# One-hot products divided over the two steps of a quad, and down products ahead of the next gates in every second step

## The reference, cut to what matters

```python
def expert_block(args):
    xb, e = args
    hid = jax.nn.silu(xb @ w_g[e]) * (xb @ w_u[e])
    return hid @ w_d[e]
```

## Time and profile before

| | us |
|---|---|
| median of 3 runs | 1539.75 (1538.67 to 1543.53) |
| the profiled execution, its own time | 1538.04 |
| its span, first to last instruction | 1536.0 |
| PE busy | 1249.5 (81%) |
| DVE busy | 654.8 (43%) |
| ACT busy | 457.5 (30%) |

### The profile page before, as it was taken

How to read it: one execution, slowest core, us unless ns; L and a number is a source line. 1 busy time by engine, 2 the same in 40 slices (tenths; PEclk the granted TensorE clock), 3 DMA queues, 4 the chain that set the end, 5 groups by cost and what they waited for, 6 DMA issues and landing times. The chain is left out here.

```text
span 1536.0 us, 21387 instructions
## 1 busy us (share of the span) xinstructions
PE 1249.5 (81%) x8548; PEld 947.1 (62%) x8548; DVE 654.8 (43%) x1369; ACT 457.5 (30%) x999; POOL 147.8 (10%) x117
## 2 busy tenths in 40 slices
PE   3799899899999739899987429978999668888871
PEld 1589655688888727665665229945899655554540
DVE  0534586364435663221210085476667652211112
ACT  1233266543342421100100145335665410100002
POOL 1301000011102320000000140000001200000002
PEclk9999989999999869999999759989999879999996
DMA  9942258732322105999999905338554229999994
GB/s 319 301 117 84 81 194 284 211 107 86 107 94 74 66 1 197 392 414 413 418 420 384 353 14 140 110 137 278 183 173 162 97 90 421 422 423 423 421 422 154
DMA packets 140762, 352.75 MB, mean 230 GB/s; under 512 B 34144, under 2 KB 95584, under 8 KB 115968
## 3 DMA queue, kind: packets, MB, share of 16 engines
q1 hardware_dynamic: 123424, 315.95, 55.7%
q10 hardware_dynamic: 14176, 24.96, 4.5%
q0 software_dynamic: 3072, 10.59, 1.8%
HBM read 329.44 MB, written 22.02 MB: 229 GB/s over the span
## 5 line engine op out<-in xcount | busy, mean ns | idle before, releaser
L1595 DVE TENSOR_TENSOR w_lo<-ring,w_hi 128x256 fp32r<-128x256 f32 x480 | 223.4, 478 | 267.0 <-ACT w_hi L1308 266.6
L1308 ACT ACTIVATE w_hi<-ring 128x256 fp32r<-128x256 f32 x480 | 197.1, 417 | 290.6 <-PE banks L852 260.2
L1073 PE MATMUL banks<-ring,arena 128*64 128x256 f32 x2048 | 233.8, 383 | 39.7 <-issue 21.7
L852 PE MATMUL banks<-h_hi,w_hi 128*128 128x512 f32 (+1 forms) x640 | 222.0, 347 | 13.8 <-DVE w_lo L1595 11.0
L1073 PEld LDWEIGHTS banks<-ring,arena 128*64 128x64 f32 x2048 | 156.5, 137 | 107.9 <-issue 35.9
L852 PE MATMUL banks<-h_lo,w_hi 128*128 128x512 f32 (+1 forms) x640 | 220.3, 344 | 0.0
L852 PE MATMUL banks<-h_hi,w_lo 128*128 128x512 f32 (+1 forms) x640 | 219.9, 344 | 0.0
L1087 PE MATMUL banks<-ring,att 128*64 128x512 f32 x512 | 118.6, 605 | 29.8 <-issue 19.8
L852 PEld LDWEIGHTS banks<-h_hi,w_hi 128*128 128x128 f32 x640 | 122.8, 192 | 30.3 <-DVE h_lo L1587 8.4
L852 PEld LDWEIGHTS banks<-h_hi,w_lo 128*128 128x128 f32 x640 | 122.8, 192 | 14.1
L852 PEld LDWEIGHTS banks<-h_lo,w_hi 128*128 128x128 f32 x640 | 122.9, 192 | 13.7
(11 more groups left out here) (186 smaller groups left out, 1648.5 us busy)
## 6 DMA issues: line engine op xcount, KB each, us to landing
ring<-in_w_e_gate SPq DMA_DIRECT2D x64, 1024.0 KB, 9.1
ring<-in_w_e_up SPq DMA_DIRECT2D x64, 1024.0 KB, 9.6
ring<-in_w_e_down SPq DMA_DIRECT2D x64, 1024.0 KB, 10.0
ring<-in_w_mod SPq DMA_DIRECT2D x48, 1024.0 KB, 5.6
ring<-in_w_in SPq DMA_DIRECT2D x38, 1024.0 KB, 8.4
expert_rows<-arena ACTq DMA_DIRECT2D x32, 512.0 KB, 8.1
ring<-in_w_o SPq DMA_DIRECT2D x8, 1024.0 KB, 5.0
ring<-in_w_branch SPq DMA_DIRECT2D x8, 640.0 KB, 4.7
```

Source lines behind the costliest of these rows:

```text
L852: ins = mm(out_ap, a, b, start=k == 0 and p_ == 0, stop=k == KD - 1 and p_ == 2)
L1073: ins = mm(banks[e * CAP:(e + 1) * CAP, bank, 0:DE], x[:, k, e * CAP:(e + 1) * CAP], w[:, k * DE:(k + 1) * DE], start=k == 0, stop=k == KD ...
L1308: fn(w_hi[:, u % AHEAD, :, :], chunk(key)[:, q * KU:(q + 1) * KU, :], ACT.Copy).then_inc(w_hi_ready, 1)
L1595: v.tensor_tensor(w_lo[:, u % AHEAD, :, :], chunk(key)[:, q * KU:(q + 1) * KU, :], w_hi[:, u % AHEAD, :, :].bitcast(F32), ALU.subtract).th ...
```

## The change

It touches `pair_step` on PE and on DVE and nothing else. The one-hot products of the next quad stood all in the even step of a quad (one ahead of the gates, two between them and the down products, one behind). Now two pieces stand in the even step and two in the odd one, both directly behind the transposes. In odd steps the down products of pair p now stand ahead of the gate and up products of pair p + 1; in even steps they stay behind them. On DVE the copies follow, and `select` for the quad after the next moves from the end of the even step to the end of the odd one. SP's and ACT's instructions keep their order.

```diff
             def pair_step(l, p, i=None):
                 d = p // 2 + 1
-                ahead = p % 2 == 0 and d < NQUAD
                 step_h(l, p, i)
-                if ahead:
-                    step_x(l, d, 0, i)
+                if d < NQUAD:
+                    step_x(l, d, 2 * (p % 2), i)
+                    step_x(l, d, 2 * (p % 2) + 1, i)
+                if p % 2:
+                    step_d(l, p, i)
                 if p + 1 < NPAIR:
                     step_gu(l, p + 1, i)
-                if ahead:
-                    step_x(l, d, 1, i)
-                    step_x(l, d, 2, i)
-                step_d(l, p, i)
-                if ahead:
-                    step_x(l, d, 3, i)
+                if p % 2 == 0:
+                    step_d(l, p, i)
...
             def pair_step(l, p, i=None):
                 d = p // 2 + 1
-                ahead = p % 2 == 0 and d < NQUAD
                 take_hidT(l, p, i)
-                if ahead:
-                    take_xT(l, d, 0, i)
+                if d < NQUAD:
+                    take_xT(l, d, 2 * (p % 2), i)
+                    take_xT(l, d, 2 * (p % 2) + 1, i)
                 if p + 1 < NPAIR:
                     take_hid(l, p + 1, i)
-                if ahead:
-                    for q in (1, 2, 3):
-                        take_xT(l, d, q, i)
-                    if d + 1 < NQUAD:
-                        select(l, d + 1, i)
+                if p % 2 and d + 1 < NQUAD:
+                    select(l, d + 1, i)
```

## The result

The changed kernel takes **1718.6 us** (median of 4 runs, 1716.1 to 1720.2), the kernel before 1541.6 us (median of 4 runs). The ratio is 1.114 (95% interval 1.110 to 1.118): slower by 177 us. Predicted were 1718 us. The profiled execution has a span of 1714.1 us, 178.1 more than before.

What follows compares the result with a forecast made beforehand. The prediction took DMA transfers to bound the expert stages. The profiled 1538.0 us plus 14 stalls of 12.76 us (178.6) gave 1716.7, and the median 1.7 above it 1718 us; own range 1700 to 1740, overall 1670 to 1760.

Steps and rivals of the forecast that it cites:

- What bounds the stage: Expert stages run at the pace of the transfers, 13.63 MB a quad at 416 to 423 GB/s.
- The drain in odd steps: DMA engines stand still from the last byte of downs(p) until gates(p+2): 12.76 us, 14 times, 178.6 us.
- the ends: At the start of the stage, new gates one piece of 2 us later; taken as 0, between -3 and +3.
- The terms of one stall: Last byte to down products 1.63, down products 3.59, gate products 3.86, issue to full rate 1.63; together 10.71 us.
- The clock: Odd steps' down products start at half speed after some 8 or 10 us idle: 2.05 us more per stall.
- Start and completion of a transfer: In each stall, 1.63 + 1.63 us by the rows; the skill page's 2.0 together would give 18 us less.
- Select hidden by the transfers: Even step: wait for select, about 2.5 us, covered by transfers; 0.9 us spare in layer 0, some 4 in layer 1.
- the drain with the clock up: Rival: odd-step stalls without cold starts, 14 x 10.71 = 150 us, total 1690 us; chance 0.17.
- The longer one: Rival: 4.5 us of slow clock instead of 2.05, plus a second drain in layer 0, 1767 us; chance 0.10.
- a second drain: Layer 0, even steps: spare 0.9 us gone, 7 x 2 us; a low window some 17 us after the first.

Runs made afterwards that it cites:

- experiment 4: Changed kernel with SP's loads in PE's new order of use (in odd steps downs of pair p ahead of gates and ups of p+1): 1567.2 us.
- experiment 5: As experiment 4, with select on DVE back at the end of the even step: 1538.9 us, ratio 0.9983 to the kernel before.
- experiments 2 and 3: 2: kernel before, only down products moved ahead of gates in odd steps, 1717.4 us; 3: changed kernel, down products first only when p % 4 == 1, 1640.9 us.
- experiment 7: Changed kernel with 952 extra unused matmuls filling PE's idle time ahead of the odd steps' down products: 1697.4 us.
- experiment 6: Changed kernel with only select on DVE moved back to the end of the even step: 1721.9 us.

## Why the prediction was right, point by point

- **What bounds the stage.** Right: with the same bytes and nearly the same PE work a quad takes 12 us longer, and experiments 4 and 5 give it back, 151 us by the order of the loads and the rest with `select`.
- **The drain in odd steps, 14 of them.** Right; experiments 2 and 3 show the cause and the count. From the first gate products to the start of the last down products, layer 0 takes 87.8 us more (348.5 against 260.7) and layer 1 93.0 more (341.2 against 248.2), against 7 x 12.76 = 89.3 predicted for each. The rest of the span is 2.8 us shorter. The prediction had both layers alike and the ends at 0; that the 3.7 us too many in layer 1 and the 2.8 too few elsewhere nearly cancel is luck.
- **The terms of one stall.** All four rightly named. In the stall shown above: the transfers end as if at 668 + (131 + 25)/426 = 668.37, the down products start 2.15 us later (1.63 predicted; a stall of layer 1, at 1553.68, had 0.9). From there to SP's issue 8.65 (7.45 plus 2.05 predicted). From the issue to the full rate 1.64 (1.63). Sum 12.44, predicted 12.76. Over all 14 stalls, reckoned in the same way, the first of these goes from 0.8 to 2.5 us and is 1.65 in the mean.
- **The clock.** From the start of the down products to SP's issue the 14 stalls take 8.46 to 10.14 us, 9.28 in the mean, so 1.83 above 7.45 where I had 2.05. But the 7.45 was too large itself: with the clock up, in the twelve fast steps of experiment 7, this stretch takes 7.23 in the mean, so that the clock costs 2.05 against them. That experiment also shows that it is the idle time that does it. In two stalls with waits of the same length, in layer 1, the products took 5.5 and 6.6 us:

```profile
1553.68 5.47 PE L1087 MATMUL banks<-ring,att 128*64 128x512 f32 x16 [10.12 <-DMA ring<-in_w_e_down]
```
```profile
1599.27 6.56 PE L1087 MATMUL banks<-ring,att 128*64 128x512 f32 x16 [10.15 <-issue]
```

  The idle times, predicted as some 8 us in layer 0 and 10 in layer 1, are 7.8 to 9.99 us in layer 0 (8.09 in the stall shown) and 9.9 to 11.0 in layer 1. The rule of the Trainium skill ("TensorE: Matmul & The Clock Gate", section "HAM oscillation — how this bites in real kernels"), that a wait for a transfer makes each next tile start cold, holds here for the long waits: by this trace every one of the 14 products in question, behind 7.8 us or more, took 4.97 us or more. Behind a wait of 2.52 us for the same kind of load, at 654.54, the down products took 3.65.
- **Start and completion of a transfer.** The page "DMA: Bandwidth & Descriptors" of the Trainium skill (section "Anatomy of one DMA — SWDGE (gpsimd) path") has 2.0 us for both; the stall shown has 2.15 + 1.64 = 3.8, that of 1553.68 with the same start about 2.5. The measurement decides: with the mean of 1.65 for the completion it is 3.3 us, as I took. The page's figure is for transfers issued from GpSimd, and no run here has one in this place.
- **Select hidden by the transfers.** Right for the changed kernel (experiment 6), though the cover was thinner than reckoned: from the issue in an odd step of layer 0 to the next one it is 14.8 to 17.4 us, where I had 15.2. The price without the cover was mis-sized in experiments 4 and 5: 28 us instead of 5 to 14. What the sum lacked are the stretches without transfers behind each wait and the half clock behind some, both in the windows of experiment 4.
- **How good the sum is.** In a single stall its terms are off in both directions: in the one shown the start was 0.5 us too small and the stretch to SP's issue 0.85 too large. In the mean of 14 they are off by 0.02 and 0.22. A single row from another place, as the prediction had for each term, does not tell a mean that well; that the total agrees within 1 us is in part luck.

The rivals: the drain with the clock up would have been 1690 us (experiment 7 made it so, for 12 of the 14 stalls: 1697). The longer one, 1767, needed a second drain in every quad of layer 0. It shows as no more than a dip: where the next issue comes latest, 17.4 us after that at 862.18, the two windows from 880 hold 295 and 246 GB/s.

## What to carry to other kernels

Where a ring of buffers is filled in a fixed order, the order of use belongs to the ring: a product moved ahead of others that were loaded earlier keeps their slots shut until its own load has landed, and the queue runs dry for the sum of all that follows until the first release. Ask of every move which slot is released last before the wait, and count from the last byte to the next full rate. If the order of use must change, change the order of the loads with it (experiment 5), and look for what the stall had covered (experiment 4).

## What the runs showed of the hardware

- Extra work made the kernel faster: 952 matmuls whose result nobody uses save 21 us, because they keep the clock from falling to half in waits of 8 to 11 us (12 of 14 down products behind them take 3.65 us, against 4.97 to 6.56 without).
- In the kernel of experiment 4 PE waits 2.5 to 2.9 us for DVE in six places of layer 0, with 0.7 us of wait and two short transposes just ahead, while the transfers run on. At three of them the granted clock fell to 0.50 at or just behind the wait, at three it stayed at 1.00. What decides this is not shown. A lowered rate of the transfers followed all six, behind the one at 706 about five microseconds later. All one-hot products together take 207 us there and 190 in experiment 5. What the wait, the clock and the lost transfers each add to the 28 us was not measured apart.
